# Two-layer hybrid backbone: scaled tokens in a place of their own, modulation slices inside the wide stage, two wide chunks in step

## The reference, cut to what matters

```python
for l in range(2):
    mod_l = silu(c) @ w_mod[l] + b_mod[l]          # 6 vectors of 1024 for latent tokens
    mod_c = silu(c_ctx) @ w_mod[l] + b_mod[l]      # the same for context tokens
    h = rms_norm(x, norm1[l]) * (1 + scale1) + shift1
    z = h @ w_in[l]                                # four branches and 4 x 1024 gate logits
    y = [retention(z), gated_linear_attention(z), grouped_attention(z), differential_attention(z)]
    x = x + gate1 * ((sum_i sigmoid(g_i) * (y_i @ w_branch[l, i])) @ w_out[l])
    h = rms_norm(x, norm2[l]) * (1 + scale2) + shift2
    u = h @ w_up[l]                                # 2 x 2816 wide
    x = x + gate2 * ((silu(conv3(u[:, :2816])) * u[:, 2816:]) @ w_down[l])
```

## Time and profile before

| | us |
|---|---|
| median of three runs | 2987.41 (2981.74 to 2996.21) |
| the profiled execution's own time | 2991.67 |
| its span in the trace | 2989.9 |
| PE busy | 2731.8 (91%) |
| POOL, DVE, ACT busy | 1522.0, 1342.2, 669.0 |
| mean granted clock of PE | 0.945 |
| in the chain that ended last | PE 79%, DVE 11%, ACT 4%, POOL 3%, DMA 2% |

### The profile page before, as it was taken

How to read it: one execution, slowest core, us unless ns; L and a number is a source line. 1 busy time by engine, 2 the same in 40 slices (tenths; PEclk the granted TensorE clock), 3 DMA queues, 4 the chain that set the end, 5 groups by cost and what they waited for, 6 DMA issues and landing times.

```text
span 2989.9 us, 37995 instructions
## 1 busy us (share of the span) xinstructions
PE 2731.8 (91%) x15620; PEld 2221.8 (74%) x15620; DVE 1342.2 (45%) x1756; ACT 669.0 (22%) x1130; POOL 1522.0 (51%) x1412
## 2 busy tenths in 40 slices
PE   5899989999988998999989997998889887899999
PEld 2688877777766886888877886786667666688877
DVE  4522066643566826555562135216643677421221
ACT  4211132221144511110020003013212245211110
POOL 2443447522412542565568524565834425488886
PEclk8899989999989998999989998999989898999999
DMA  7422412311311821333433362221212116333322
GB/s 244 134 66 89 116 31 62 87 38 50 106 38 40 256 72 57 113 113 113 121 103 111 91 205 55 83 68 49 65 50 61 46 36 208 88 92 98 94 89 80
DMA packets 361592, 277.84 MB, mean 93 GB/s; under 512 B 10139, under 2 KB 322111, under 8 KB 360908
## 3 DMA queue, kind: packets, MB, share of 16 engines
q1 hardware_dynamic: 359040, 272.57, 30.7%
q10 hardware_dynamic: 1612, 2.75, 0.2%
q0 software_dynamic: 768, 0.09, 0.0%
HBM read 246.01 MB, written 29.36 MB: 92 GB/s over the span
## 4 chain that ended last, share of the span: by engine, by line
PE 79%; DVE 11%; ACT 4%; POOL 3%; DMA 2%; issue 2%; SPq 0%; DVEq 0%; ACTq 0%; POOLq 0%
PE ps L445 18%; PE ps L446 17%; PE ps L447 17%; PE ps L664 4%; PE ps L990 3%; PE ps L595 2%; PE ps L484 2%; PE ps L486 2%; PE ps L485 2%; POOL w_hi L1127 1%; PE ps L684 1%; POOL w_lo L1130 1%; PE ps L626 1%; DVE arena L1695 1%; PE ps L791 1%
## 5 line engine op out<-in xcount | busy, mean ns | idle before, releaser
L1127 POOL TENSOR_TENSOR w_hi<-ring,tiny 128x512 fp32r<-128x512 f32 x516 | 592.2, 1148 | 1196.9 <-PE ps L447 659.5
L445 PE MATMUL ps<-hh,w_hi 128*128 128x512 f32 (+1 forms) x2272 | 852.6, 375 | 45.1 <-DVE hl L1665 24.7
L1130 POOL TENSOR_TENSOR w_lo<-ring,w_hi 128x512 fp32r<-128x512 f32 (+1 forms) x572 | 790.1, 1382 | 104.8 <-ACT w_hi L1291 64.4
L446 PE MATMUL ps<-hl,w_hi 128*128 128x512 f32 (+1 forms) x2272 | 826.2, 364 | 0.0
L447 PE MATMUL ps<-hh,w_lo 128*128 128x512 f32 (+1 forms) x2272 | 824.2, 363 | 0.0
L445 PEld LDWEIGHTS ps<-hh,w_hi 128*128 128x128 f32 x2272 | 446.4, 196 | 158.7 <-issue 56.9
L447 PEld LDWEIGHTS ps<-hh,w_lo 128*128 128x128 f32 x2272 | 445.2, 196 | 65.5
L446 PEld LDWEIGHTS ps<-hl,w_hi 128*128 128x128 f32 x2272 | 447.4, 197 | 60.2 <-issue 1.7
L1271 ACT ACTIVATE arena<-ps 128x512 f32<-128x512 f32 (+3 forms) x130 | 76.0, 584 | 442.2 <-PE ps L447 430.8
L484 PE MATMUL ps<-w_hi,hh 128*128 128x256 f32 (+1 forms) x544 | 157.6, 290 | 11.8 <-ACT arena L1271 11.8
L445 PE MATMUL ps<-ffh,w_hi 128*128 128x512 f32 x352 | 143.5, 408 | 19.2 <-POOL w_lo L1130 12.8
(11 more groups left out here) (242 smaller groups left out, 3849.7 us busy)
## 6 DMA issues: line engine op xcount, KB each, us to landing
ring<-in_w_in SPq DMA_DIRECT2D x118, 512.0 KB, 4.1
ring<-in_w_mod SPq DMA_DIRECT2D x96, 512.0 KB, 4.0
ring<-in_w_up SPq DMA_DIRECT2D x88, 512.0 KB, 4.3
ring<-in_w_down SPq DMA_DIRECT2D x48, 512.0 KB, 4.0
logits<-arena SPq DMA_DIRECT2D x32, 384.0 KB, 2.3
arena<-logits SPq DMA_DIRECT2D x32, 384.0 KB, 3.6
ring<-in_w_down SPq DMA_DIRECT2D x24, 384.0 KB, 3.4
ring<-in_w_branch SPq DMA_DIRECT2D x16, 512.0 KB, 4.5
```

The source lines that it names most:

```text
L445: pe.matmul(acc, wh[:, k], hi[:, n, x:y], start=n == 0, stop=False)
L446: pe.matmul(acc, wh[:, k], lo[:, n, x:y], start=False, stop=False)
L1127: pool.tensor_tensor(wh[:, 0:count], w, one[:].unsqueeze(2).to_broadcast([P, count, P]), ALU.mult).then_inc(*up("w_lead", ("lead", key, j)))
L1130: pool.tensor_tensor(wl[:, 0:count], w, wh[:, 0:count].bitcast(F32), ALU.subtract).then_inc(*up("w_split", ("split", key, j)))
```

## The change

Five edits. (1) The scaled tokens get a place of their own (`x_scaled`, in what was `xn`), so `xin` stays; the turned scaled tokens go to `xT` at first. The plain tokens are no longer turned in the opening but inside the first product: after the three matmuls of k-tile n PE turns tile n, and ACT alone copies it into `xT`, between its `hh` tiles. The mask is made after the first scaled tile, and ACT's decay factors after the second group of the modulation. (2) Between: `turned` stands behind the slot's projection instead of `before` it, ACT's bias moves to the next even slot, groups 5 and 7 use bank 6. (3) Layer 1's 48 slices all stand in the wide stage, spread over 44 chunks (chunks 0, 11, 22, 33 have two). (4) The sums over partitions are made inside a chunk's second half, two after each k-tile's three matmuls, with chunks 7, 14, 22, 29, 36; the last stays in the narrow stage. (5) Chunks 0 and 1 of the wide stage are computed in step, k-tile by k-tile, in both layers; POOL splits them as a pair.

```diff
+def slices_with(l, c):
+    slices = next_modulation(l)
+    return [key for n, key in enumerate(slices) if n * 2 * FT // len(slices) == c]
+def vector_summed_with(c):
+    return {8 * (g + 1) * 2 * FT // 48: g for g in range(5)}.get(c)
...
         for c in range(2 * FT):
-            order += [("up", l, c)] + slices[c:c + 1]
+            order += [("up", l, c)] + slices_with(l, c)
         for n in range(3 * KT):
-            order += [("down", l, n // 3, n % 3)] + slices[2 * FT + n:2 * FT + n + 1]
+            order += [("down", l, n // 3, n % 3)]
...
-        xn = arena[:, 16 * T:24 * T].rearrange("p (k t) -> p k t", t=T)
+        x_scaled = arena[:, 16 * T:24 * T].rearrange("p (t d) -> p t d", t=NT)
+        xn = xT
+        tb_first = arena[:, 16 * T:18 * T].rearrange("p (b t) -> p b t", b=2)
...
-                    mm = pe.matmul(acc, wl[:, k], hi[:, n, x:y], start=False, stop=n == whole - 1)
+                    mm = pe.matmul(acc, wl[:, offset + k], hi[:, n, x:y], start=False, stop=n == whole - 1)
+                    if each and key == ("f", 0, "ret", 0):
+                        turn_tokens("x", n)
...
+                        if summed is not None and j == 1:
+                            if x == 0:
+                                begin_sum(key[1] + 1, summed, (banks[0] + 4) % 8, (banks[0] + 4) % 8 + 1)
+                            for k in range(KT // 2):
+                                mm = product(acc[:, x:y], key, j, hi, lo, x, y, count=1, first=KT // 2 + k, offset=k)
+                                part_of_sum(key[1] + 1, summed, (KT // 2 if x else 0) + k)
...
+            def two_projections(keys, width, banks_of, each):
...
+                for j in range(2):
+                    for key in keys:
+                        pe.wait_ge(*at(("split", key, j)))
+                    for k in range(KT // 2 * j, KT // 2 * (j + 1)):
+                        for key in keys:
+                            for x, y in ends:
+                                mm = product(psum(key)[:, x:y], key, j, hh, hl, x, y, count=1, first=k, offset=k - KT // 2 * j,
+                                             each=each if key == keys[0] and x == 0 else None)
+                            if k % (KT // 2) == KT // 2 - 1:
+                                mm.then_inc(*up("pe_half", ("half", key, j), *([("full", key)] if j else [])))
...
-                bank = g if g < 4 else 7
+                bank = modulation_bank(g)            # g < 4: g; 5 and 7: bank 6; else 7
...
+            def begin_sum(l, g, *banks):
...
+                pe.wait_ge(*at(("used", ("slice", l, g, KT - 1))))
+            def part_of_sum(l, g, m):
+                key = ("mods", l, g)
+                for s in range(2):
+                    mm = pe.matmul(psum(key)[:, 2 * m + s:2 * m + s + 1], mod_sum[:, s, m * P:(m + 1) * P], one, start=True, stop=True)
...
-            for k in range(KT):
-                turn_tokens("x", k)
...
-                        if slot is not None:
-                            before(b, slot)
...
                             projection(("f", l, b, j), hh, hl, W[l] if is_q(b, j) else T, banks(), each=each)
+                            turned(b, j)
                             behind(b, j)
...
-                for c in range(2 * FT):
+                two_projections([("up", l, 0), ("up", l, 1)], W[l], [(0, 1), (2, 3)], lambda k: ("hl", l, 2, k))
+                for c in range(2, 2 * FT):
                     projection(("up", l, c), hh, hl, W[l], (2 * (c % 4), 2 * (c % 4) + 1),
-                               each=(lambda k: ("hl", l, 2, k)) if c == 0 else None)
-                    if l + 1 < DEPTH and c % KT == 0 and c > 0:
-                        sum_of_modulation(l + 1, c // KT - 1, 2 * ((c + 3) % 4), 2 * ((c + 3) % 4) + 1)
+                               summed=vector_summed_with(c) if l + 1 < DEPTH else None)
...
+            def tokens_again(k):
+                act.wait_ge(*at(("scaled", 0, 1, k)))
+                act.wait_ge(*at(("hh", 0, 1, k)))
+                tokens_out("x", xT, k)
...
                         ins.then_inc(*up("lead_ready", ("hh", l, which, k)))
+                        if k >= 1:
+                            tokens_again(k - 1)
+                    tokens_again(KT - 1)
...
-            dve.wait_ge(*at(("full", ("x", KT - 1))))
             for t in range(NT):
-                dve.tensor_scalar(xin[:, t], xin[:, t], token_root[:, t:t + 1], None, ALU.mult).then_inc(*up("token_scaled", ("xn_in", t)))
+                dve.tensor_scalar(x_scaled[:, t], xin[:, t], token_root[:, t:t + 1], None, ALU.mult).then_inc(*up("token_scaled", ("xn_in", t)))
...
                     step(right, "dve_free", ("free", key))
-                    if l + 1 < DEPTH:
-                        modulation_step(l + 1, 2 * c // KT, 2 * c % KT)
+                    for key in slices_with(l, 2 * c):
+                        modulation_step(*key[1:])
```

More of the change, by code:

```diff
@@ L436, in next_chunk, with product @@
                 used[0] += 1
-            def product(acc, key, j, hi, lo, x, y, count=KT // 2, first=0, whole=KT, each=None):
+            def product(acc, key, j, hi, lo, x, y, count=KT // 2, first=0, whole=KT, each=None, offset=0):
                 wh, wl = w_halves(key, j)
@@ L459, in projection @@
                             pe.wait_ge(*at(("split", key, j)))
[L460 to L461 removed]
+                        if summed is not None and j == 1:
[4 more added lines that the diff above has]
+                                part_of_sum(key[1] + 1, summed, (KT // 2 if x else 0) + k)
+                        else:
+                            mm = product(acc[:, x:y], key, j, hi, lo, x, y, first=KT // 2 * j,
+                                         each=each if each and (x == 0) == (each(0)[2] != "ctx") else None)
                         if (x, y) == ends[-1]:
                             mm.then_inc(*up("pe_half", ("half", key, j), *([("full", key)] if j else [])))
+            def two_projections(keys, width, banks_of, each):
+                ends = segs(width)
+                for key, banks in zip(keys, banks_of):
+                    next_chunk(key)
+                    for s, n in room(key, *banks):
+                        pe.wait_ge(s, n)
+                for j in range(2):
[8 more added lines that the diff above has]
+                                mm.then_inc(*up("pe_half", ("half", key, j), *([("full", key)] if j else [])))
             def token_projection(l, b, pair):
@@ L504, in modulation_turned @@
             def modulation_turned(g):
-                for s, n in room(("mt", g), g if g < 4 else 7):
+                for s, n in room(("mt", g), modulation_bank(g)):
                     pe.wait_ge(s, n)
@@ L866, in _, with turned @@
                     modulation_turned(3)
-                def before(b, slot):
+                def turned(b, slot):
                     if slot % 2 == 0 and 0 < slot // 2 <= len(columns_between(l)[b]):
@@ L906, in _ @@
                     for pair in token_pairs(b)[lag // 2:]:
-                        slot = nf + pair[0] // 2
-                        before(b, slot)
                         token_projection(l, b, pair)
-                        behind(b, slot)
-                    for slot in (nf + nt - nt // 2, nf + nt - nt // 2 + 1):
-                        before(b, slot)
+                        turned(b, nf + pair[0] // 2)
+                        behind(b, nf + pair[0] // 2)
                     if b in BEFORE:
@@ L1137, in split_until @@
                     first = split_chunks[done[0]]
-                    pair = next(p for p in token_pairs(first[2]) if first[3] in p) if first[0] == "t" else (0,)
+                    if first[0] == "t":
+                        pair = next(p for p in token_pairs(first[2]) if first[3] in p)
+                    else:
+                        pair = (0, 1) if first[0] == "up" and first[2] == 0 else (0,)
                     split(*split_chunks[done[0]:done[0] + len(pair)])
```

67 lines of the change are left out of this document (37 added, 30 removed).

## The result

The changed kernel takes 3006.68 us (median of 6 runs, 2995.53 to 3012.62), the kernel before on the same chip 2989.59 us (6 runs, 2981.74 to 2998.59): ratio 1.0047, 95% interval 1.0028 to 1.0066. It is slower by half a per cent, clear of the noise; 2979 was forecast, with 3001 as the upper end of the range. The profiled execution took 3003.51 us (span 3000.8) against 2991.67 (span 2989.9): 11.8 us more, with the spans 10.9 apart.

What follows compares the result with a forecast made beforehand. PE was taken as the bound, 79% of the chain. Terms from opening to narrow stage summed to -8.8 us on the median 2987.41, giving 2978.6, say 2979; the range for 8 in 10 was 2955 to 3001.

Steps and rivals of the forecast that it cites:

- the term of the sums: Layer 0's wide stage: late slices stop PE in chunks 7 and 29, +10.3 us; spreading holds the clock, -8.4 us.
- Doubles: Layer 0's wide stage: double slices at 11, 22, 33 make PE wait before chunks 12 and 34, +16.4 us.
- The start of the wide stage: First two chunks in step: layer 1 gains 5.6 us; layer 0 loses 4, PE idling 11 us before chunk 2.
- Opening: Start through first product: `hh` 9.4 us earlier, product 10 us longer, 1.7 of lower clock; +2 us in all.
- retention branch: Turned groups no longer make PE wait there, first rotation 17.8 us earlier; -17 us taken, range -20 to -11.
- R3: Rival, opening: the turns in the first product hide in it, -10 us, total 2969; chance 0.12.
- begins at 115.4: Retention branch: start of the token pair behind the turned group, at 115.4 us instead of 133.8.
- R4: Rival: ACT's and DVE's strips hold the retention branch as before, its 17 us gain becomes 5, total 2991; chance 0.12.
- Narrow stage: Layer 0: without slices PE resumes some 2 us earlier, one POOL instruction still standing until about 1566; -6 us.
- R5: Rival, narrow stage: POOL gets in between DVE's residuals, PE never waits, 6 us more gained, total 2973; chance 0.08.
- R1: Rival, layer 0's wide stage: the ring's doubles and slices don't hold PE, total 2949; chance 0.12.
- R2: Rival: the wide stage is paced by its own loop of slice, load and split, +24 us, total 3003; chance 0.13.

Runs made afterwards that it cites:

- E9: E3 with two slices behind chunks 11 and 18, two instead of four in the narrow stage; 2981.91 us, ratio 0.9969 to the kernel before.
- E10: The changed kernel, doubles kept, with each sum in one block behind its chunk and no mid-chunk wait; 2983.61 us, ratio 0.9980 to the kernel before.
- E3: The changed kernel with one slice behind each wide chunk, the last four in the narrow stage, sums still spread; 2965.10 us, ratio 0.9914 to the kernel before.
- E2: The changed kernel with the mid-chunk wait kept but the 16 small products in one block behind the chunk; 2998.52 us, ratio 1.0016 to the kernel before.
- E6: E3 with the first two wide chunks of each layer one behind the other, not in step; 2963.42 us, ratio 0.9899 to the kernel before.
- E4: The changed kernel with layer 0's 3 MB residual write issued behind the retention branch's last token weight load; ratio 1.0033 to the kernel before.
- E7: The kernel before with only the turned groups moved behind the projection, their bias later, groups 5 and 7 in bank 6; 2979.30 us, ratio 0.9938.
- E1: The changed kernel with each sum's 16 small products all in the chunk's last 256 columns; 2989.95 us, ratio 0.9988 to the kernel before.
- E8: The changed kernel with single slices, four behind output projections and 44 behind wide chunks, sums spread, residual write later; 2949.87 us, ratio 0.9854 to the kernel before.
- E5: E3 with each sum's 16 small products in one block behind its chunk; 2972.70 us, ratio 0.9925 to the kernel before.

## Why the prediction was wrong

**The step that failed** is the term of the sums: "3.1 idle and 1.7 of clock, twice", with "Spread, I expect the clock to hold". The waits came as read (3.18 and 3.06), and in 14, 22 and 36 the clock held. But in chunks 7 and 29 the clock cost 8.2 and 8.2, not 1.7: the price of one short spell, taken from a chunk of plain products behind a block, was applied to a stretch in which small products stand between the large. Plain products behind a wait come near that price (2.0 and 1.7 us behind the stops of 5.50); these do not. The two edits, "the sum asks for a slice that is late" and "the sum is spread", were priced each by itself; it is their meeting that costs. Forecast for the sums +1.9, measured +13.1. E9 made one such meeting (14.8), E10 and E3 took them away (5.2 and 3.6 a sum). E10 and E3 take the wait and the meeting away together; E2 keeps the wait and shows that with plain products behind the wait the clock comes back sooner, once clearly and once half.

**Doubles: right in kind, one term missed.** The stops before 12 and 34 are 5.50 each (5.9 said) with 2.0 and 1.7 of clock (2.3 said). "up23 comes behind an odd chunk ... nothing" was right for chunk 23 and passed over 24: both chunks behind a double take a slice's place, and up24 takes that of the first slice behind chunk 22, an even one. DVE and SP show it:

```profile
1362.38 1.42 DVE L1639 TENSOR_SCALAR rope<-ring,tiny 128x1024 f32<-128x1024 f32 x2
1363.83 0.38 SPq L1117 DMA_DIRECT2D ring<-in_w_up  x1
```

That slice is used 5 us after the end of chunk 22, which the sum spread in it had itself put off by 3.5; behind a block the stop is absent (E10). +20.7 instead of +16.4. E9 put a double at an odd and one at an even chunk, and the stops came at the successors that this reading names.

**The start of the wide stage.** Chunk 2 waits 11.80 (11 said) and costs +5.2 over before with its clock (+4 said); layer 1 gains 5.7 (5.6). E6 gives 5.2 and 5.6 for the two layers by themselves.

**Opening and retention branch.** `hh` 8.9 earlier (9.4), from there to the end of the first product 26.6 us (28.5 was the estimate): the term was sound, R3 is out. (Of the +2 forecast 1.7 were to fall behind that end.) In the retention branch the turned groups cost nothing any more, but the load of the token weights was left out of the sum: SP issues the residual's 3 MB at 95.65, just ahead of them, and before, where it was issued at 96.28, the next loads of `w_in` followed only at 117.45 (now 105.23), held back with PE by the very waits that went. The step "begins at 115.4" is 6 us too early, and of -17 came -9.5. What is late next was a transfer and not ACT's strips (R4); E4 shows it. The stretch up to the wide stage gained 12.0 instead of 4.5. That this makes up for the 7.5 us missing before it is luck: where a profiled execution reaches the wide stage varies by as much (E7).

**Narrow stage: right in size (-7.5, -6 said), wrong in the way.** I expected one POOL instruction still to stand for 12 us. It did not; the rows that answer to the earlier trace rows:

```profile
1568.85 1.38 POOL L1182 TENSOR_TENSOR w_hi<-ring,tiny 128x512 fp32r<-128x512 f32 x1 [3.31 <-DMA ring<-in_w_down]
1569.25 11.31 DVE L2108 TENSOR_TENSOR ffl<-arena,ffh 128x512 fp32r<-128x512 f32 x9
1570.31 1.61 POOL L1185 TENSOR_TENSOR w_lo<-ring,w_hi 128x512 fp32r<-128x512 f32 x1
1580.70 0.47 PE L459 MATMUL ps<-ffh,w_hi 128*128 128x512 f32 x1 [0.82 <-DVE ffl L2108]
```

POOL's instructions take 1.4 to 1.6 us in between DVE's, which take 1.26 each on average instead of 0.6, and inside the stage PE waits 0.8 at most. This is R5's picture without its price: 12 us were said for it. By the Trainium skill, "SBUF — State Buffer", section "Who interferes with whom", each of the two blocks the other for its whole instruction; these rows agree with that. With the slices back (E3), the same POOL instruction begins 1.5 us behind the first residual and stands for 12.73 us through all 22 again, which that rule does not say:

```profile
1522.55 13.32 DVE L2108 TENSOR_TENSOR ffl<-arena,ffh 128x512 fp32r<-128x512 f32 x22
1524.04 12.73 POOL L1182 TENSOR_TENSOR w_hi<-ring,tiny 128x512 fp32r<-128x512 f32 x1 [4.83 <-DMA ring<-in_w_down]
```

In the six profiled executions without slices here (the changed kernel, E1, E2, E4, E8, E10) POOL begins between 0.4 us ahead of the first residual and 0.4 behind it, and the form is the short one; in the six with slices (before, E3, E5, E6, E7, E9) 1.2 to 1.9 us behind, and it is the long one. That moment alone does not decide. In the narrow stage of layer 1, where no run has slices and that part of the program is the same in all, both forms occur, and with the short one POOL begins 5.2 us behind the first residual. Timeline of POOL there in E3 (first residual at 2827.81) and E5 (at 2838.66):

```profile
2832.99 1.36 POOL L1182 TENSOR_TENSOR w_hi<-ring,tiny 128x512 fp32r<-128x512 f32 x1 [3.10 <-PE ps L461]
2845.26 8.98 POOL L1183 TENSOR_TENSOR w_hi<-ring,tiny 128x512 fp32r<-128x512 f32 x1 [4.51 <-PE ps L461]
```

There the short form came in three of the twelve (E1, E3, E7: 5.2, 5.2 and 6.1 us behind), the long one in nine (6.1 to 6.6 behind). What decides stays open.

**Layer 1, +4.9 that nobody forecast.** From its gated branch (2046.76 before) to its wide stage nothing is changed, and the time differs. Windows of this stretch before and after:

```profile
2046.76:2605.23 558.47, 484.52 (x2687) 366.11 (x2687) 322.59 (x439) 166.23 (x283) 276.79 (x291) 0.93 0.27 79
```
```profile
2055.95:2620.28 564.33, 487.82 (x2686) 369.30 (x2687) 320.71 (x439) 166.01 (x283) 276.33 (x291) 0.92 0.27 78
```

In the experiments the same stretch takes 557.4 (E1) to 569.5 us (E3), and 568.9 in the fastest kernel of all (E8), so this is scatter of a stretch with many short waits, not an effect of the change. The granted clock goes with it: 0.93 over the stretch before and in E1, 0.91 in E3 and E8. The profiled execution before stands near its short end, which makes the changed kernel look some us worse than it is.

R1 (the ring does not hold) and R2 (the whole loop paces) did not happen: chunks without a double or a late sum take 8.36, as before. That R2's 3003 lies near the measured 3006.68 is chance. The forecast's sum missed the profiled pair by 20 us; 17.5 of it is the wide stage of layer 0: 11.2 the sums, 4.3 the doubles, 1.2 the start, 0.8 the last chunk.

## What to carry to other kernels

Price a wait together with what the waiting engine does behind it: a spread sum cost 14.8 us with a wait of 3 us ahead of it, and 3.6 where nothing was late. In a ring that is shared by transfers with different users, follow for each load whose place it takes: two in a row of the slow user hurt both loads behind them (5.5; 2.0 and 2.3 us), and four of them in an earlier stage, behind the output projections, cost nothing there (E8). When a wait goes, look at the loads issued in its shadow, not only at the engines.

## What the runs showed of the hardware

Small products (128x1, float32) between large ones: 16 of them cost 3.5 us and leave the granted clock at 1.00 (chunk 14, and all five in E3); the same 16 in one block cost 3.5 and a dip behind (0.83 in the next chunk, E5); spread behind a wait of 3 us they ran at the low level of 1.2 GHz through the half chunk (0.70 and 0.67 over the chunk), although PE had work without a gap there. Spread twice as dense, over the last 256 columns, they left the clock at 1.00 in two chunks and brought a dip in a third without a wait (E1). And one POOL instruction beside a row of DVE's with two inputs was seen in both forms, 1.4 us between them and 12.7 us until their end; in layer 1 both forms came from the same program (1.36 us in E3, 8.98 in E5).
